# Inverting the delta rule's triangles with VectorE transposes, and two reordered product streams, in a three-layer kernel

## What is computed

```python
lower = jnp.where(strict, jnp.einsum('nbhcd,nbhsd->nbhcs', kb, k) * decay, 0.0)
sol = lax.linalg.triangular_solve(eye + lower, rhs, left_side=True, lower=True, unit_diagonal=True)
u, w = sol[..., :Dh], sol[..., Dh:]
intra = jnp.einsum('nbhcd,nbhsd->nbhcs', q, k) * decay
...
tail = lax.cumsum(log_1m_beta, axis=3, reverse=True) - log_1m_beta
a = jnp.where(before, jnp.exp(log_beta + tail), 0.0)
```

## Time and profile before

| | us |
|---|---|
| median of three runs | 2124.94 (2124.16 to 2127.75) |
| profiled execution | 2125.2 |
| its span, first to last instruction | 2123.1 |
| TensorE busy | 2070.0 |
| VectorE busy | 1088.1 |
| ACT busy | 753.4 |
| POOL busy | 219.9 |

### The profile page before, as it was taken

The page is one execution under the profiler, slowest core; times in us unless marked ns, Lnnn a source line. Parts: engine busy times, 40 slices in busy tenths (PEclk is TensorE's granted clock), DMA queues, the critical chain, the costliest instruction groups (busy, mean ns, idle before and its releaser), DMA issues.

```text
span 2123.1 us, 28504 instructions
## 1 busy us (share of the span) xinstructions
PE 2070.0 (97%) x11649; PEld 1714.7 (81%) x11649; DVE 1088.1 (51%) x1397; ACT 753.4 (35%) x1040; POOL 219.9 (10%) x196
## 2 busy tenths in 40 slices
PE   7999999999999999989999999999999999999998
PEld 7887788888888888866888888888787878888886
DVE  4764665554454453354554354456676435354453
ACT  6444432532222341475522222231574243222221
POOL 3000220400000040000400000141302010000001
PEclk9999999999999999999999999999999999999999
DMA  6231001222222322101132222334222212222221
GB/s 248 79 115 45 21 22 39 82 100 99 99 86 92 119 80 99 41 21 73 67 111 88 99 99 99 119 114 138 96 80 80 100 40 96 98 89 93 99 99 60
DMA packets 28336, 186.99 MB, mean 88 GB/s; under 512 B 3536, under 2 KB 3664, under 8 KB 6480
## 3 DMA queue, kind: packets, MB, share of 16 engines
q1 hardware_dynamic: 25200, 173.48, 22.8%
q0 software_dynamic: 2320, 11.01, 1.5%
q10 hardware_dynamic: 720, 1.11, 0.1%
HBM read 181.39 MB, written 2.10 MB: 86 GB/s over the span
## 4 chain that ended last, share of the span: by engine, by line
PE 91%; DVE 5%; ACT 3%; DMA 1%; issue 1%; ACTq 0%; DVEq 0%
PE PS L571 89%; ACT Y L1473 1%; DVE Y L2187 1%; DVE WL L2190 1%; ACT WH L1473 1%; DVE Y L2190 1%; DVE SQ L2190 0%; DMA STG<-weights 0%; DMA MX<-mem_t 0%; PE PS L789 0%; PE PS L598 0%; ACT ABUF L1473 0%; ACT SQ L1473 0%; DVE QKV L2190 0%; DVE HL L2190 0%
## 5 line engine op out<-in xcount | busy, mean ns | idle before, releaser
L571 PE MATMUL PS<-HH,WH 128*128 128x512 f32 x1544 | 608.4, 394 | 6.3 <-DVE HL L2190 4.1
L571 PE MATMUL PS<-HH,WL 128*128 128x512 f32 x1544 | 601.9, 390 | 0.0
L571 PE MATMUL PS<-HL,WH 128*128 128x512 f32 x1544 | 591.5, 390 | 0.0
L2190 DVE TENSOR_TENSOR WL<-STG,WH 128x2048 fp32r<-128x2048 f32 (+1 forms) x159 | 358.6, 2255 | 264.5 <-ACT WH L1473 264.4
L1473 ACT ACTIVATE WH<-STG 128x2048 fp32r<-128x2048 f32 (+2 forms) x167 | 307.2, 1839 | 522.6 <-PE PS L571 520.6
L571 PEld LDWEIGHTS PS<-HH,WH 128*128 128x128 f32 x1544 | 290.3, 188 | 71.6 <-DVE HL L2190 5.8
L571 PEld LDWEIGHTS PS<-HH,WL 128*128 128x128 f32 x1544 | 290.4, 188 | 60.4
L571 PEld LDWEIGHTS PS<-HL,WH 128*128 128x128 f32 x1544 | 290.5, 188 | 59.6 <-issue 0.7
L571 PE MATMUL PS<-UPH,WH 128*128 128x512 f32 x832 | 324.3, 390 | 1.4 <-DVE UPL L2187 1.4
L571 PE MATMUL PS<-UPH,WL 128*128 128x512 f32 x832 | 323.9, 389 | 0.0
L571 PE MATMUL PS<-UPL,WH 128*128 128x512 f32 x832 | 323.8, 389 | 0.0
(11 more groups left out here) (319 smaller groups left out, 2087.8 us busy)
## 6 DMA issues: line engine op xcount, KB each, us to landing
STG<-weights SPq DMA_DIRECT2D x159, 1024.0 KB, 4.8
KEY_STG<-weights POOLq DMA_DIRECT2D x4, 1024.0 KB, 6.1
XT<-x_t SPq DMA_DIRECT2D x2, 1024.0 KB, 9.1
KEY_X<-mem_t POOLq DMA_DIRECT2D x2, 1024.0 KB, 6.3
out_t<-Y SPq DMA_DIRECT2D x8, 256.0 KB, 2.0
STG<-weights SPq DMA_DIRECT2D x4, 256.0 KB, 5.4
MX<-mem_t ACTq DMA_DIRECT2D x4, 256.0 KB, 7.6
CON<-consts SPq DMA_DIRECT2D x1, 1024.0 KB, 8.9
```

Source lines behind the costliest of these rows:

```text
L571: return pe.matmul(o, l, r, start=start, stop=stop, **kw)
L2190: return dve.tensor_tensor(o, a, b, op)
```

## The change

In `prepare`, TensorE makes the three mask products first and the three spreads behind them; it makes all off-diagonal products before the attention products. VectorE interleaves the triangles, the low corners and the first levels. Level 0's set is gone: VectorE subtracts BT from the identity into XTr and transposes it in blocks of 32x32 into XX. In levels 1 to 4 the second set YT x XTr is gone: XTr is XX transposed by VectorE in blocks of 32x32 (up to level 4 the inverse has no entries outside these blocks on the diagonal). Level 5 keeps both sets; its upper corners are subtracted after all low ones. `between` is moved by one level: for group 0 decay and key rows 0 in level 2, value rows 0 and key rows 1 in 3, value rows 1 and key rows 2 in 4, value rows 2 in 5; for group 1 decay and norm sums in 2, key and value rows 3 in 3, norm rows 0, key rows 4, value rows 4 in 4, key rows 5 and norm rows 1 in 5, and value rows 5 and norm rows 2 in a new place 6, between the two products of the low corner. ACT's value copies move with them. The memset of `keys` and the last product of `gated` for heads 0 to 2 go to POOL. A.out sums three tiles together over k. `tails` makes the triangular products first, those of the diagonal blocks next and TAIL's last. In layer C two semaphores become one.

```diff
-                elif lv >= 2:
-                    pool.wait_ge(sems["lv_y"], 21 * g + 3 * (lv - 2) + e + 1)
-                if lv == 2:
+                elif lv == 2:
                     pool.wait_ge(sems["lv_x"], 18 * g + e + 1)
+                elif lv > 2:
+                    pool.wait_ge(sems["lv_y"], 18 * g + 3 * (lv - 3) + e + 1)
...
+    def zero_corners(g):
+        pool.wait_ge(sems["bt"], 18 * g + 18)
+        for n in range(3 * g, 3 * g + 3):
+            pool.wait_ge(sems["kr_mm"], n + 1)
+            pool.memset(chunks(QKV[64:P, 6 + n, :])[:, :, 0:64], 0.0).then_inc(sems["zeroed"], 1)
...
+    for n in range(3):
+        pool.wait_ge(sems["t1"], n + 1)
+        pool.tensor_tensor(QKV[:, n, :], QKV[:, n, :], GATES[n][:, :], ALU.mult).then_inc(sems["gated0"], 1)
...
-                spread(PS[:, 3 + e, :], 0, 3 * g + e, False)
-                mm(PS[:, 3 + e, :], LATE[:, :], IDENT4[:, :], False, True).then_inc(sems["spread"], 1)
+                mm(PS[:, 3 + e, :], LATE[:, :], IDENT4[:, :], True, False)
+            for e in range(3):
+                spread(PS[:, 3 + e, :], 0, 3 * g + e, False).then_inc(sems["spread"], 1)
...
         def invert(g, between):
 
-            for lv in range(6):
+            for lv in range(1, 6):
                 for e in range(3):
                     pe.wait_ge(sems["bt"], 18 * g + 3 * lv + e + 1)
-                    if lv:
-                        pe.wait_ge(sems["lv_x"], 18 * g + 3 * lv + e - 2)
-                    corners(3 + e, 0, BT[e][lv % 2], XX[e] if lv else None).then_inc(sems["lv_y"], 1)
-                if lv == 0:
-                    continue
+                    pe.wait_ge(sems["lv_x"], 18 * g + 3 * lv + e - 2)
+                    corners(3 + e, 0, BT[e][lv % 2], XX[e]).then_inc(sems["lv_y"], 1)
                 between(lv)
                 for e in range(3):
                     pe.wait_ge(sems["lv_yc"], 18 * g + 3 * lv + e - 2)
                     if lv == 1:
                         pe.wait_ge(sems["at"], 3 * g + e + 1)
-                    corners(e, 0, XTr[e], YT[e])
-                    corners(e, 256, YT[e], XTr[e]).then_inc(sems["lv_p"], 1)
+                    pe.wait_ge(sems["lv_t"], 21 * g + 3 * lv + e - 2)
+                    last = corners(e, 0, XTr[e], YT[e])
+                    if lv == 5:
+                        last = corners(e, 256, YT[e], XTr[e])
+                    last.then_inc(sems["lv_p"], 1)
...
     def norms_beside(n):
+        if n == 0:
+            norm_sums(1, 4)
         if n == 1:
-            norm_sums(1, 4)
-        if n == 3:
-            norm_rows(3, 2)
-            norm_rows(4, 3)
-            norm_rows(5, 4)
+            norm_rows(3, 3)
+            norm_rows(4, 4)
+        if n == 2:
+            pe.wait_ge(sems["gated"], 1)
+            norm_rows(5, 5)
+
+    def out_beside_norms(u, order):
+
+        def step_k(v, j, n):
+            k, bank = order[n], PS[:, 2 * (v % 2) + j, :]
+            wh, wl = WH[v % 2][:, k, j * P:(j + 1) * P], WL[v % 2][:, k, j * P:(j + 1) * P]
+            mm(bank, wh, HH[:, k, :], n == 0, False)
+            mm(bank, wh, HL[:, k, :], False, False)
+            last = mm(bank, wl, HH[:, k, :], False, n == KD - 1)
+            if n == KD - 1:
+                last.then_inc(sems["tile"], 1)
+
+        pe.wait_ge(sems["lo"], u + 2)
+        for n in range(KD):
+            pe.wait_ge(sems["hl"], split_done("A.mix", n))
+            step_k(u, 0, n)
+            step_k(u, 1, n)
+            step_k(u + 1, 0, n)
+            norms_beside(n)
+        for n in range(KD):
+            step_k(u + 1, 1, n)
+        for v in range(u + 2, u + NU["A.out"]):
+            product(v, None, 0, HH, HL)
...
+            pe.wait_ge(sems["sb_sp"], n + 1)
+            for o, w in ((0, 3 * P), (5 * P, 3 * P)):
+                mm(PSF[:, SB_BASE[e] + o:SB_BASE[e] + o + w], con("neg_tri"), SP[e][:, o:o + w], False, False,
+                   skip_group_check=True)
+            pe.wait_ge(sems["sb_m"], n + 1)
+            for o, w in ((3 * P, P), (4 * P, P), (8 * P, 2 * P)):
+                mm(PSF[:, SB_BASE[e] + o:SB_BASE[e] + o + w], con("neg_tri"), SP[e][:, o:o + w], False, True,
+                   skip_group_check=True)
+            for h in range(2):
+                if c == 0:
+                    mm(stick_block(n, h, 2), con("neg_ones"), SP[e][:, sb_at(h, 3):sb_at(h, 3) + P], False, True,
+                       skip_group_check=True)
+                else:
+                    mm(stick_block(n, h, 1, 2), con("neg_ones"), diagonals(SP[e])[:, h, :, :], False, True,
+                       skip_group_check=True)
             pe.wait_ge(sems["sb_t"], n + 1)
             for h in range(2):
-                if c == 0:
-                    mm(stick_block(n, h, 0, 2), con("neg_ones"), TAIL[:, e, 256 * h:256 * h + 256], False, False,
-                       skip_group_check=True)
-                    mm(stick_block(n, h, 2), con("neg_ones"), SP[e][:, sb_at(h, 3):sb_at(h, 3) + P], False, False, skip_group_check=True)
-                else:
-                    mm(stick_block(n, h, 0), con("neg_ones"), TAIL[:, e, 256 * h:256 * h + P], False, False,
-                       skip_group_check=True)
-                    mm(stick_block(n, h, 1, 2), con("neg_ones"), diagonals(SP[e])[:, h, :, :], False, False,
-                       skip_group_check=True)
-            for o, w in ((0, 512), (512, 512), (1024, 256)):
-                last = mm(PSF[:, SB_BASE[e] + o:SB_BASE[e] + o + w], con("neg_tri"), SP[e][:, o:o + w], False, True,
+                w = 2 if c == 0 else 1
+                last = mm(stick_block(n, h, 0, w), con("neg_ones"), TAIL[:, e, 256 * h:256 * h + w * P], False, True,
                           skip_group_check=True)
...
+            def triangle(e):
+                dve.wait_ge(sems["kq_mm"], 6 * g + e + 1)
+                for o in (0, 64):
+                    last = tt(chunks(LTC[e][o:o + 64]), chunks(PS[o:o + 64, 3 + e, 0:256]), corner(DT[e], o), ALU.mult)
+                last.then_inc(sems["lt"], 1)
+
+            def attention(e):
+                dve.wait_ge(sems["kq_mm"], 6 * g + 3 + e + 1)
+                tt(AT[e], PS[:, e, :], DT[e], ALU.mult).then_inc(sems["at"], 1)
+
+            def first_level(e):
+                dve.wait_ge(sems["bt"], 18 * g + e + 1)
+                tt(chunks(XTr[e]), four(IDC), chunks(BT[e][0]), ALU.subtract).then_inc(sems["lv_t"], 1)
+                dve.wait_ge(sems["lv_t"], 21 * g + e + 1)
+                dve.transpose(XX[e], XTr[e]).then_inc(sems["lv_x"], 1)
+
+            def low_corner(e):
+                tt(chunks(LOFF[e]), chunks(PS[0:64, 3 + e, 256:512]), off_corner(DT[e]), ALU.mult)
+
+            triangle(0)
+            triangle(1)
+            low_corner(0)
+            triangle(2)
+            first_level(0)
+            low_corner(1)
+            first_level(1)
+            low_corner(2)
+            first_level(2)
             for e in range(3):
-                n = 3 * g + e
-                dve.wait_ge(sems["kq_mm"], 2 * n + 1)
-                for o in (0, 64):
-                    tt(chunks(LTC[e][o:o + 64]), chunks(PS[o:o + 64, 3 + e, 0:256]), corner(DT[e], o), ALU.mult)
-                tt(chunks(LOFF[e]), chunks(PS[0:64, 3 + e, 256:512]), off_corner(DT[e]), ALU.mult).then_inc(sems["lt"], 1)
+                attention(e)
+
+        def level(g, lv):
+
+            def subtracted(e):
+                dve.wait_ge(sems["lv_p"], 18 * g + 3 * lv + e - 2)
+                tt(XX[e], XX[e], PS[:, e, 0:256], ALU.subtract).then_inc(sems["lv_x"], 1)
+
+            def turned(e):
+                dve.wait_ge(sems["lv_x"], 18 * g + 3 * lv + e + 1)
+                dve.transpose(XTr[e], XX[e]).then_inc(sems["lv_t"], 1)
+
+            subtracted(0)
+            subtracted(1)
+            turned(0)
+            subtracted(2)
+            turned(1)
+            turned(2)
+
+        def last_level(g):
+
+            def inverse_corner(e, o):
+                return tt(corner(QKV[:, 6 + 3 * g + e, :], o), chunks(XTr[e][o:o + 64]),
+                          chunks(PS[o:o + 64, e, 256:512]), ALU.subtract)
+
             for e in range(3):
-                n = 3 * g + e
-                dve.wait_ge(sems["kq_mm"], 2 * n + 2)
-                tt(AT[e], PS[:, e, :], DT[e], ALU.mult).then_inc(sems["at"], 1)
-
-        def first_level(g):
+                dve.wait_ge(sems["lv_p"], 18 * g + 15 + e - 2)
+                tt(XX[e][0:64], XX[e][0:64], PS[0:64, e, 0:256], ALU.subtract).then_inc(sems["lv_x"], 1)
+                inverse_corner(e, 64).then_inc(sems["lv_t"], 1)
             for e in range(3):
-                dve.wait_ge(sems["lv_y"], 21 * g + e + 1)
-                tt(chunks(XX[e]), four(IDC), chunks(PS[:, 3 + e, 0:256]), ALU.subtract)
-                tt(chunks(XTr[e]), four(IDC), chunks(BT[e][0]), ALU.subtract).then_inc(sems["lv_x"], 1)
-
-        def level(g, lv):
-            for e in range(3):
```

(42 more changed lines are left out.)

## The result

The changed kernel takes 2105.65 us in the median of four runs (2101.44 to 2106.97). The kernel before took 2125.95 us beside it; the ratio is 0.9904, with a 95% interval of 0.9888 to 0.9919. The profiled execution took 2105.53 us with a span of 2103.7, which is 19.4 us less than the span of before. The forecast was 2106.0.

A forecast was written before the change was run, and what follows sets the result against it. TensorE, busy 97% of 2123.1 us, was taken as the bound. Gains of 7.8 (group 0), 6.4 (group 1), 4.5 (A.out) and 3.0 (stick-breaking) less 2.4 (clock) made 19.3 us: 2125.2 to 2106 us, range 2098 to 2116.

The forecast's parts named there:

- group 0: First inversion of the delta rule, start to solve: 7.8 us gained, solve at 258.95 instead of 266.76.
- group 1, at full clock: Second inversion of the delta rule: 6.4 us gained, solve at 326.05 instead of 332.42, clock booked separately.
- A.out: First output layer: TensorE's 2.65 us wait for HL goes, and the half clock behind it: 4.5 us gained.
- stick-breaking, at full clock: Stick-breaking stage: TAIL waits go, a ring through ACT then sets 13.34 us per pair: 3.0 us, between 1.5 and 4.1.
- clock elsewhere: Clock term: one or two more spells at half clock, 1.6 us each, expected after the change: -2.4 us.
- a ring: Inversion levels: loop through TensorE's sets and VectorE's subtracts, turns and `keys`, 4.9 us a level instead of 5.66.
- The entry: Start of a group, reordered products: in group 0 level 2 starts at 236.75 instead of 241.60, 4.85 us sooner.
- (1): Rival: VectorE's turns are dear, 0.69 us each; 8.7 us are lost, giving 2114.6; chance 0.15.
- (2): Rival: half clock all through the inversions, five more spells than counted, 8 us, giving 2114; chance 0.12.
- (3): Rival: TensorE stays the bound, VectorE is done before it asks, no new spell; about 2099.6 us; chance 0.10.
- (4): Rival: slower than before, a turn stalls VectorE; decides from 1.07 us a turn, 2129 at 1.2; chance 0.05.
- (5): Rival: TAIL's and HL's idle time returns one step later, levels save nothing; 2118 to 2122 us; chance 0.06.

The follow-up runs named there:

- the filler's run: Changed kernel, with eight unread spreads made by TensorE in group 1 where it waits for `keys(5)`: 2101.34 us, ratio 0.9893.
- the change again: The changed kernel once more, unedited: 2107.56 us, ratio 0.992.
- entry undone: Changed kernel with TensorE's old entry order: mask and spread alternate, each off-diagonal product is followed by its attention product; VectorE unchanged: 2108.84 us, ratio 0.9918.
- products undone: Changed kernel with each head's attention products again behind its off-diagonal products at the entry; masks stay ahead of spreads: 2111.72 us, ratio 0.9933.
- inversions alone: Changed kernel with A.out and `tails` put back as before, leaving only the delta rule's part: 2114.31 us, ratio 0.9944.
- without the three tiles: Changed kernel with only the A.out edit undone: 2111.98 us, ratio 0.9937.

## Why the prediction was right

Its total was right and its terms were nearly so. That it hit 2105.65 within 0.4 us is luck: the same kernel again has a median of 2107.56, and its executions lie between 2101 and 2109. As the traces have it, group 1 with its way to A.out gave 5.0 and not 6.4, and stick-breaking 4.6 and not 3.0, and the two cancelled. Since the prediction booked the clock as a term of its own, the measured gains have to be freed of the clock before they are compared:

| term | predicted | measured | of it |
|---|---|---|---|
| group 0 | 7.8 | 7.5 | |
| group 1, at full clock | 6.4 | 6.5 | 5.03 and the clock's 1.5 |
| A.out | 4.5 | 4.5 | forecast as 2.9 wait, 1.6 clock |
| stick-breaking, at full clock | 3.0 | 3.4 | 4.63 less 1.2 |
| clock elsewhere | -2.4 | -1.9 | -1.5, +1.2, -1.6 |
| ahead of group 0 | 0 | -0.6 | |

**Group 0.** The mechanism was right: a ring, of 4.77 us where `keys` alone stands in it (predicted 4.9, before 5.66) and 5.37 with `queries` of head 2. The difference is the turn, which costs 0.33 in the ring and not 0.38: 3 x 0.05 makes 4.75. The head start grew from 3.28 us at level 1 to 4.74 at level 2 (predicted 4.85), 5.96 at level 4 (5.65), 6.85 at level 5 (6.4) and 7.54 at the solve. The levels gave 0.3 to 0.45 us more than I took, and the last level gave 0.7 where I took 1.4; these two errors nearly cancelled. The entry was right in sum, and the runs have split its 3.28 us at level 1: 1.96 for the product order, 0.33 for the mask order, 1.0 for level 0 and VectorE's order. The gain of the mask order has a source that I did not name: products of a kind follow each other sooner, 0.3 us and not 0.42. The first off-diagonal product starts 3.61 us behind the start of the group; I had it at 3.42, and before it was 3.90.

**Group 1.** At full clock it is 6.5 us against 6.4. The working of that number: the filler's run shows that the lower clock costs 2.07 us ahead of the solve and 1.07 behind it, 3.14 together. Before, the same way from the solve to A.out took 16.88 us, 1.62 more than the filler's 15.26. So without the clock the two are 66.28 and 59.73. The idle times of 0.8, 0.8, 2.2 and 1.6 us in levels 2 to 5 were 0.44, 0.48, 1.56 and 1.08, and the wait for `keys(5)` 2.05 and not 2.5; each was put too large, and the places were right. What the step lacked is the tie between two of its own numbers: it knew of a wait of 2.5 us, knew of the earlier trace rows that a wait of 2.65 us had been followed by the lower clock, and still booked the clock as "one or two more spells" at no place. The spell came right behind that wait, lasted 6.8 us, not 3.4, and cost 3.1 and not 1.6. As the spell that lay behind the solve before had cost 1.6, the net loss there was 1.5.

**A.out** was right to a tenth, and the run without it gives 4.6; wait and clock are both gone, but no run parts their shares of 2.9 and 1.6. The weight split of the third unit, which I named as the next thing late, was in time: TensorE has no idle time in the window.

**Stick-breaking.** Two terms were mis-sized in opposite directions. A pair takes 13.08 us and not 13.34, since I closed the ring with the log's length (1.36 us and a hand-over) where ACT starts the next operation 1.27 us behind the log's start; the row for that, 908.32 to 909.59 in the trace of before, was at hand. That is 0.57 us a pair, 2.8 in five, and not 1.5. The end gave only 0.63 (from the last pair's AW to the next projection 8.71 us, before 9.34), where I had hoped for 1.5. The sum of 3.4 lies within my bounds of 1.5 to 4.1.

**The rivals.** (1) fell by the turns themselves: 0.33 us, the lower end of my bounds, and of the twelve in the levels of a group ten are paid. (2) named the right place and the wrong number: one spell, twice as long, and in four other traces three times. (3) is half true: over the kernel TensorE is still the bound, in a level it isn't, with 3.17 us of idle time in group 0. (4) would have needed 1.07 us a turn; even with every turn of the levels made twice the kernel stays at 0.994. (5) is wrong for A.out and stick-breaking and right for group 1 alone, where the wait did move, from the levels to the place ahead of the solve.

What stays open is where the other stretches at the lower clock come from. The change had a new one at 1371 in one trace and at 1570 in the next, in code that it doesn't touch. Of the one at 1371 the trace shows that it came behind a wait of 0.66 us, which the trace of before has as well (at 1391) without it. The one at 746 is not new: before had it at 762, and the change again did not. No run here was made for them.

## What to carry to other kernels

When work is taken off the bounding engine inside a loop over two engines, write the loop out as a ring with one number per hand-over, and take the start-to-start distance of two operations, not their lengths; then ask for each piece whether it lies ahead of the engine that closes the ring or in the gap behind it, for only in the gap is it free. When the sum contains a new wait of TensorE of some 2 us, book a stretch at half clock at that place as likely: here it came in seven traces of nine and cost one and a half times the wait in the change. The repair is cheap: let the waiting products go behind some that are ready, or fill the wait.

## What was new about the hardware

- A block transpose of 128x256 float32 on VectorE lasts 0.42 us in the mean and costs 0.33 in a row of operations, the same as a subtract of that size. By the Trainium skill (VectorE: DVE Perf Modes, The three transpose paths) I had an estimate of 0.44: that is the length of a single one here, but a poor price for the ring.
- The clock fell to the lower level at the end of group 1 in seven of nine traces with a TensorE wait of 2.05 to 2.09 us there, from 0.9 us ahead of the wait's end to 1.9 behind it, and in none of three in which the wait was filled with eight products or removed. It fell behind three of four waits of 1.86 us (entry undone, both groups; products undone, group 1) and within 1.2 us behind each of three waits of 2.65 us in A.out (before, inversions alone, without the three tiles). It stayed up in group 0 of the change, whose 3.17 us of idle time come in pieces of at most 0.54. The Trainium skill (TensorE: Matmul & The Clock Gate, A second HAM failure mode) blames frequent short idle times between groups of products; the traces agree where the clock fell behind short waits alone (332.42 before, 292.6 with the wait filled), but here short ones mostly did nothing, and a single long one mostly did.
- The lower clock lasts longer than the wait that brings it: 6.8 or 10.2 us for one of 2.1. In the change all 6.8 us lay behind the wait, in products that ran at half speed.
